# Feed-forward steps of a two-block transformer kernel: from activations standing to weights standing, with four products of 512 columns ahead of four of 256 in each block

## The reference

```python
def swiglu(x, w_gate, w_up, w_down):
    return (jax.nn.silu(x @ w_gate) * (x @ w_up)) @ w_down
...
def swiglu_ffn(x, g, w_gu, w_down):
    h = rms_norm_2(x, g)
    ...
    return (jax.nn.silu(gate) * up) @ w_down
```

## Time and profile before

| what | value |
|---|---|
| median of 3 runs | 1708.65 us (1708.61 to 1708.91) |
| the profiled execution: its own time | 1708.45 us |
| its span, first to last instruction | 1706.3 us |
| TensorE products (PE) | busy 99% of the span |
| weight loads into the array (PEld) | 81% |
| VectorE (DVE), ScalarE (ACT) | 60%, 49% |
| GpSimd (POOL) | 6% |

### The profile page before, as it was taken

The page is one execution under the profiler, slowest core; times in us unless marked ns, Lnnn a source line. Parts: engine busy times, 40 slices in busy tenths (PEclk is TensorE's granted clock), DMA queues, the critical chain, the costliest instruction groups (busy, mean ns, idle before and its releaser), DMA issues.

```text
span 1706.3 us, 22051 instructions
## 1 busy us (share of the span) xinstructions
PE 1694.1 (99%) x8308; PEld 1374.5 (81%) x8308; DVE 1022.8 (60%) x1481; ACT 840.0 (49%) x1102; POOL 109.1 (6%) x141
## 2 busy tenths in 40 slices
PE   8999999999999999999999999999999999999999
PEld 6888887788888888878778888888888787788887
DVE  6444756754556454769866545554547698665454
ACT  5444565643454343566664434443435666644342
POOL 2000200200003000100011000020001010110000
PEclk9999999999999999999999999999999999999999
DMA  8555542455557555534344554565555344345542
GB/s 296 184 202 176 173 173 99 166 193 196 180 190 232 195 185 184 197 107 159 131 136 170 189 197 175 195 229 198 176 192 195 104 156 138 129 171 194 197 172 99
DMA packets 69805, 299.87 MB, mean 176 GB/s; under 512 B 5408, under 2 KB 7680, under 8 KB 44512
## 3 DMA queue, kind: packets, MB, share of 16 engines
q1 hardware_dynamic: 66752, 291.52, 49.1%
q0 software_dynamic: 2688, 7.19, 1.4%
q10 hardware_dynamic: 288, 0.10, 0.0%
HBM read 297.74 MB, written 1.05 MB: 175 GB/s over the span
## 4 chain that ended last, share of the span: by engine, by line
PE 98%; DVE 1%; ACT 0%; DMA 0%; issue 0%; POOL 0%; ACTq 0%
PE ps L547 13%; PE ps L545 13%; PE ps L546 13%; PE ps L609 9%; PE ps L611 9%; PE ps L610 9%; PE ps L818 6%; PE ps L820 6%; PE ps L819 6%; PE ps L566 2%; PE ps L567 2%; PE ps L593 2%; PE ps L908 1%; PE ps L986 1%; PE ps L353 1%; PE ps L569 1%
## 5 line engine op out<-in xcount | busy, mean ns | idle before, releaser
L260 DVE TENSOR_TENSOR w_lo<-raw,w_hi 128x2048 fp32r<-128x2048 f32 x275 | 625.0, 2291 | 217.0 <-ACT w_hi L253 216.8
L253 ACT ACTIVATE w_hi<-raw 128x2048 fp32r<-128x2048 f32 x275 | 520.5, 1913 | 59.7 <-PE ps L820 32.5
L545 PE MATMUL ps<-w_hi,aT_hi 128*128 128x512 f32 x960 | 379.4, 395 | 0.0
L547 PE MATMUL ps<-w_hi,aT_lo 128*128 128x512 f32 x960 | 374.6, 390 | 0.0
L546 PE MATMUL ps<-w_lo,aT_hi 128*128 128x512 f32 x960 | 373.9, 389 | 0.0
L703 ACT ACTIVATE tmp<-ps,stats 128x256 f32<-128x256 f32 x132 | 62.6, 474 | 578.9 <-PE ps L547 568.6
L746 DVE TENSOR_TENSOR tmp<-tmp,ps 128x256 f32<-128x256 f32 x132 | 55.6, 421 | 337.4 <-ACT tmp L703 337.2
L609 PE MATMUL ps<-w_hi,act_hi 128*128 128x512 f32 x576 | 226.7, 394 | 0.1
L611 PE MATMUL ps<-w_hi,act_lo 128*128 128x512 f32 x576 | 224.4, 390 | 0.0
L610 PE MATMUL ps<-w_lo,act_hi 128*128 128x512 f32 x576 | 224.3, 389 | 0.0
L547 PEld LDWEIGHTS ps<-w_hi,aT_lo 128*128 128x128 f32 x960 | 180.2, 188 | 38.4
(11 more groups left out here) (296 smaller groups left out, 1605.5 us busy)
## 6 DMA issues: line engine op xcount, KB each, us to landing
raw<-in_ffn_units SPq DMA_DIRECT2D x197, 1024.0 KB, 5.0
raw<-in_w_in SPq DMA_DIRECT2D x34, 1024.0 KB, 5.2
raw<-in_w_gate SPq DMA_DIRECT2D x24, 1024.0 KB, 5.2
raw<-in_w_out SPq DMA_DIRECT2D x12, 1024.0 KB, 4.9
qk_t<-in_nsa_cmp_w POOLq DMA_DIRECT2D x8, 512.0 KB, 5.8
raw<-in_w_br_b SPq DMA_DIRECT2D x4, 1024.0 KB, 5.1
raw<-in_w_br_a SPq DMA_DIRECT2D x2, 1024.0 KB, 4.8
raw<-in_w_br_c SPq DMA_DIRECT2D x2, 1024.0 KB, 5.6
```

Of the source, the lines that this page charges most:

```text
L253: nc.scalar.activation(w_hi[w][:, :], raw[k][:, :], ACT.Copy).then_inc(hi_ready, 1)
L260: nc.vector.tensor_tensor(w_lo[w][:, :], raw[k][:, :], w_hi[w][:, :].bitcast(F32), ALU.subtract)\
L545: nc.tensor.matmul(dst, aT_hi[:, a, toks], hi[:, k, :], start=a == 0, stop=False)
L547: last = nc.tensor.matmul(dst, aT_lo[:, a, toks], hi[:, k, :], start=False, stop=a == KC - 1)
```

## The change

Step 0 of each part stays as it is. In steps 1 to 10 the roles are exchanged:

- A block is 128 hidden columns of gate or of up; a step has four (gate, up, gate, up), each with a bank of its own. The weights stand in the array, and the activations of all 256 tokens move. `aT` now holds both parts side by side, so one product with `w_hi` moves 512 columns (256 of `aT_hi`, 256 of `aT_lo`), and one with `w_lo` moves the 256 of `aT_hi`. For each half of the channels a block has four products of 512 and then four of 256.
- The bank then holds `hi*hi + lo*hi` and `hi*lo` side by side. DVE adds the two halves with a reduction (`summed`), which also brings them into SBUF.
- The result already has hidden columns on the partitions: no transposes, but for those of step 0. `rstd` now varies along the free axis, so once per part it is turned into rows of 256 numbers (`pe_rstd_rows`, a copy by ACT), and DVE multiplies the gate by it.
- The four banks of a step are the same in each step (4 to 7; in step 1 it is 2, 3, 6, 7). So TensorE waits at the start of a step until all four blocks of the last have been summed (`gu_summed`), and in step 1 the down product of tile 1 waits for the blocks in banks 2 and 3.
- In `pe_pv` the second key tile's product comes ahead of the first's.

```diff
-        def pe_gate_up(pe, n, slot, par, t, kh):
...
-            for k in range(KC // 2):
-                a = kh * (KC // 2) + k
-                nc.tensor.matmul(dst, aT_hi[:, a, toks], hi[:, k, :], start=a == 0, stop=False)
-                nc.tensor.matmul(dst, aT_hi[:, a, toks], lo[:, k, :], start=False, stop=False)
-                last = nc.tensor.matmul(dst, aT_lo[:, a, toks], hi[:, k, :], start=False, stop=a == KC - 1)
+        def pe_gate_up(pe, ph, s, like, between=None):
+            u0, n0 = ph["u0"], ph["n0"]
+            if like != 1:
+                pe.wait_ge(gu_summed, 4 * s + 4 * n0)
+            for kh in range(2):
...
+                for j, c in enumerate((0, STEP_F, P, STEP_F + P)):
+                    dst = gu_bank(like, j)
+                    for k in range(KC // 2):
+                        a = kh * (KC // 2) + k
+                        nc.tensor.matmul(dst, hi[:, k, c:c + P], aT[:, :, a, :], start=a == 0, stop=a == KC - 1,
+                                         skip_group_check=True)
+                    for k in range(KC // 2):
+                        a = kh * (KC // 2) + k
+                        mm = nc.tensor.matmul(dst[:, 0, :], lo[:, k, c:c + P], aT_hi[:, a, :], start=False,
+                                              stop=a == KC - 1, skip_group_check=True)
...
+        def pe_rstd_rows(pe, ph):
+            for t in range(NT):
+                wait_rstd(pe, ph, t)
+                last = nc.tensor.transpose(ps[:, RSTD_BANK, t * P:(t + 1) * P],
+                                           rstd(ph, t).broadcast_to([P, P]), ident)
...
+            def summed(dst, f, j):
+                wait_block(dve, ph, s, j)
+                bank = gu_bank(like, j)
+                nc.vector.tensor_reduce(dst[:, f, :], bank.rearrange("p w s -> p s w"), AX.X, ALU.add)\
+                    .then_inc(gu_summed, 1)
+                dve.wait_ge(gu_summed, 4 * s + (4 * ph["n0"] + j + 1))
+            def gate(f):
+                summed(gate_t, f, 2 * f)
+                nc.vector.tensor_tensor(gate_t[:, f, :], gate_t[:, f, :], rstd_rows, ALU.mult).then_inc(gate_scaled, 1)
+            def up(f):
+                summed(up_t, f, 2 * f + 1)
+                dve.wait_ge(silu_ready, 2 * s + (2 * s0 + f + 1))
+                nc.vector.tensor_tensor(up_t[:, f, :], up_t[:, f, :], gate_t[:, f, :], ALU.mult).then_inc(act_ready, 1)
```

More of the change, by code:

```diff
@@ L592, in pe_act_transposes, with wait_block @@
+                mm.then_inc(unit_used, 1)
+                if kh == 0 and between:
+                    between()
+        def wait_block(eng, ph, s, j):
+            if j < 3:
+                eng.wait_ge(gu_done, 3 * s + (3 * ph["n0"] + j + 1))
+            else:
+                eng.wait_ge(unit_used, 3 * s + (ph["u0"] + 1))
+        def pe_act_transposes(pe, ph, t):
+            pe.wait_ge(act_ready, 2 * ph["s0"] + t + 1)
             for f in range(2):
-                last = nc.tensor.transpose(act_t_psum(par, t)[:, f, :], sg[par][:, t, f * P:(f + 1) * P], ident)
+                last = nc.tensor.transpose(act_t_psum(t)[:, f, :], sg[:, t, f * P:(f + 1) * P], ident)
@@ L621, in pe_down @@
             pe.wait_ge(act_lo_ready, 2 * s + 2 * ph["s0"])
-            pe_rows(pe, n, (3 * like + ph["u0"] + 1) % W_SLOTS, act_hi[par], act_lo[par], 0, first, False)\
-                .then_inc(unit_used, 1)
+            if first:
+                pe.wait_ge(rstd_rows_ready, ph["ffn_before"] + 1)
+            for t in range(NT):
+                if first and t == 1:
+                    pe.wait_ge(gu_summed, 4 * (ph["n0"] + 1) + 2)
+                mm = pe_rows(pe, n, (3 * like + ph["u0"] + 1) % W_SLOTS, act_hi[par], act_lo[par], 0, first, False, (t,))
+            mm.then_inc(unit_used, 1)
         def next_of(ph):
@@ L700, in split @@
                     split_hi(act, n)
[L702 to L710, removed]
@@ L711, in act_step @@
-            if first:
-                wait_rstd(act, ph, 0)
-            else:
-                split(1)
-            act.wait_ge(gu_t0_done, s + (s0 + 1))
-            silu(0)
[L717 to L721, removed]
-            act.wait_ge(unit_used, 3 * s + (u0 + 1) if not first else u0 + 2)
-            if first:
-                wait_rstd(act, ph, 1)
+            if not in_loop and s == 0:
+                wait_rstd(act, ph, 0)
+                act.wait_ge(gu_t0_done, ph["ffn_before"] + 1)
+                for t in range(NT):
+                    if t:
+                        act.wait_ge(unit_used, u0 + 2)
+                        wait_rstd(act, ph, 1)
+                    nc.scalar.activation(sg[:, t, :], gu(t)[:, 0, :], ACT.Silu, scale=rstd(ph, t)).then_inc(silu_ready, 1)
+                return
@@ L725, in act_step @@
+            split(2)
+            split(3)
+            silu(0)
+            hi(0)
             silu(1)
+            hi(1)
             if last:
-                hi(s, par, 0)
-            if not first:
-                split(3)
-            if last:
-                hi(s, par, 1)
                 split_hi(act, ph["u_end"] + 1)
@@ new lines, in dve_step @@
+            split(1)
+            if like == 1:
+                for t in range(NT):
+                    dve.wait_ge(act_hi_ready, 2 * s0 + t + 1)
+                    toks = slice(t * P, (t + 1) * P)
+                    nc.vector.tensor_tensor(act_lo[0][:, :, toks], act_t_psum(t), act_hi[0][:, :, toks].bitcast(F32),
+                                            ALU.subtract).then_inc(act_lo_ready, 1)
+                dve.wait_ge(rstd_rows_ready, ph["ffn_before"] + 1)
+            split(2)
+            dve.wait_ge(act_lo_ready, 2 * s + 2 * s0)
@@ L764, in dve_step @@
+            gate(0)
+            if like != 1 and not last:
+                split(3)
+            up(0)
+            if like == 1:
+                split(3)
+            gate(1)
+            lo(0)
+            up(1)
+            lo(1)
             if last:
-                lo(s, par, 0)
-            if not first:
                 split(3)
-            if last:
-                lo(s, par, 1)
                 split_lo(dve, ph["u_end"] + 1)
@@ L983, in pe_pv @@
                 pe.wait_ge(att_pt_dve if hh else att_pt_act, B + 1)
-            for kt in range(NT):
+            for kt in (1, 0):
                 for hh in range(2):
```

104 lines of the change are left out of this document (52 added, 52 removed).

## The result

The change takes 1703.28 us (1703.04 to 1704.11), the kernel before 1708.63: a ratio of 0.9969, 95% interval 0.996 to 0.9978. It is faster by 0.3%; 0.8% was forecast, and the time lies 0.3 us outside the range. One of the eight runs of the kernel before was a slow one (1873.42 us), and the ratio is of fast runs alone. The profiled execution has a span of 1701.3 us.

The account below looks back on a forecast made before the run. TensorE's own products were taken as the bound. Savings of 14.6 (loop steps) and 3.1 (ends), less 2.6 (step 1) and 1.4 (opening stalls), make 13.7 us off 1708.45: 1694.75, median 1695.0 us; range 1692 to 1703.

Parts of the forecast that it names:

- the switch back from 256 to 512: In gate and up, eight times a step: taken to cost 0, bounded from above by 0.11 us each.
- the forecast step: Steps 2 to 10: 11.09 us gate and up plus 5.44 down, kept as 16.54 us, against 16.81 before.
- The rival that the switch costs: Switch from 256 back to 512, 480 times: at 0.03 us each 1709 us, at 0.11 us 1748; chance 0.05.
- The other rivals for the loop: Among them, products of 256 not covering their operand load: 2.2 us more a step, 1829 us; chance 0.03.
- the gap behind a wait: First two products behind a wait, 0.34 us apart against 0.2267: gave the switch back's upper bound of 0.11 us.
- the forecast's own signs of being wrong: A loop step over 16.7 us, reductions near 1 us, or PE waiting in the loop.
- The sign for the step: Loop steps: the forecast counts as wrong if one takes over 16.7 us, where 16.54 was forecast.
- The opening stall: Start of step 2 in each part: TensorE waits for DVE's last reduction, 0.21 to 0.25 us; six cost 1.4 us.
- the rival of longer hand-overs: Opening and end: 0.1 us more per link between engines or dependent operations, giving 1701 us; chance 0.2.
- Step 1 up to its down product: Step 1's gate and up products with six transposes at 0.71 us: 11.81 us.
- The end: End of each part: two pairs of transposes go, 0.52 us, 3.1 us in six; `act_lo` in time with 0.46 us slack.
- One price of a rival: Reduction at 1.36 us, twice the forecast: 26 us lost, 1721 us, loop still holding with 0.3 us slack; chance 0.08.

Follow-up runs that it names:

- far order: The change with all 16 products of 512 in a half of the channels, then its 16 of 256 (reversed in the second half of steps 2 to 9): 1696.32 us.
- strict alternation: The change with each product of 512 followed at once by its product of 256, 32 returns a step: 1709.19 us, ratio 1.0004 to the kernel before.
- pairs: The change with the products of two blocks gathered, 8 of 512 and then 8 of 256, so 4 returns a step: 1703.03 us.
- groups of two: The change with two products of 512, then two of 256, and so on, 16 returns a step: 1698.26 us, ratio 0.9941 to the kernel before.

## Why the prediction was wrong

**The step that failed** is the sentence on the switch back from 256 to 512: "I take 0". Gate and up come to 11.20 us instead of 11.09, nine times a part, and the down product behind them to 5.47 or 5.49 instead of 5.44, eight times: 0.99 + 0.38 = 1.37 us a part, 8.2 us in six. The miss is 8.3 us (1703.28 less 1695.0); that the two agree so well is chance, as the other terms below show, but this one is by far the largest. It was shown by moving products alone: the far order gave the forecast step, the strict alternation ate the gain. The rival that the switch costs was named, with a chance of 0.05 and a price of 0.03 us each for no gain; spread over 480 returns the measured cost is 0.017. The other rivals for the loop did not come up. A bound looked for in one row, the gap behind a wait, was the wrong kind of row: the cost lies in the distances of the five to nine products behind it, and the earlier trace rows were read for one distance only.

None of the forecast's own signs of being wrong came up: a step took 16.70 us and not more, the reductions 0.69, and PE did not wait in the loop. The sign for the step was too wide: 0.16 us over the forecast in each of 60 steps is 9.6 us, more than the range allows.

**The opening stall** was forecast at 0.21 to 0.25 us and took 0.40: 6 x 0.17 = 1.0 us. The last reduction came at 17.45 instead of 17.29. DVE's own chain, from the split to that reduction, took 8.61 us, the forecast's 8.65; it began 0.20 late, because ACT was busy when its copy fell due and because DVE followed ACT by 0.10 us and not 0.03. PE then started 0.14 us behind DVE, not 0.06. So the rival of longer hand-overs was right in two links between engines, not in the waits of DVE for itself.

**The other terms.** Step 1 up to its down product: 5.59 + 0.57 + 5.69 = 11.85 us, forecast 11.81 (the six transposes took 0.57, not 0.71, and the products more). Its down product took 0.03 us more without the stall (5.47). The end: 0.47 us less, forecast 0.52; `act_lo` came in time, and pairs showed how little was to spare. The reduction: 686 ns, forecast 680. Silu reads SBUF now and takes 420 ns, forecast 474; the copy for `act_hi` 419, forecast 380. The loop's chain on DVE hid as forecast. The attention loop: nothing, as forecast. Step 1 and the end make another 0.7 us in six parts, so the terms come to 8.2 + 1.0 + 0.7 = 9.9 us, 1.6 more than the miss. Some 0.9 us of it came back between the parts (0.1 to 0.3 us each time, of which no term of the forecast speaks; why was not followed up). Another 0.4 us is that the time of an execution lies 1.97 us over its span in the change and 2.15 before, and that the profiled execution of the change is at its median and not 0.2 below. The rest is rounding. One price of a rival does not follow from its own numbers: with a reduction of 1.36 us the loop's slack of 2.7 us is used up by 4 x 0.68 = 2.7, and 0.3 us is not left. Nothing hung on it.

The forecast rested on the rows. The Trainium skill (TensorE: Matmul & The Clock Gate, Back-to-back issue gap) has a formula for an isolated product, by which one of 256 columns would be estimated at 109.2 ns. The far order, with 32 in a row, has 120, so the trace does not agree. The Trainium skill (TensorE: Matmul & The Clock Gate, The mechanism) also says that a load overlaps running products only when the row group differs. Here too the trace does not agree: in the far order 32 loads of 0.19 us, all over 128 rows, start every 0.12 us beside the products.

The kernel gains less than it could because of its order, not because of the roles: with the orders of TensorE and of DVE's step 1 changed, the forecast's 1695 is reached and passed (1693.94).

## What to carry to other kernels

Where TensorE is the bound and products of two widths are mixed, gather those of one width as far as the banks and the engines behind allow, and read the distances of all the products behind a change of width, not the first alone: 15 ns for eight products is 0.5% of the whole. Halfway gathering is no sure gain: groups of two (a step of 16.60 us) beat groups of four and of eight (16.70, 16.63), and they let each block complete as early as in the change, so a few lengths are worth a run. Before gathering, ask which block becomes complete later and who waits for it: at the end of a part 0.90 us of delay against 0.46 us of slack ate the whole gain of gathering pairs. And a wait that is added between steps has its cost where the engine behind it catches up, in the first step; there, put the long operation that is not yet due last.

## What the runs showed of the hardware that was not expected

Products of 512 columns behind products of 256 are longer than 227 ns, five of them where nothing disturbs them (233, 236, 228, 233, 231) and nine behind the transposes of the kernel before; in strict alternation single ones reach 241. The first products of 256 behind wide ones are shorter than 120 (113, 119). It does not depend on how the moving operand lies (one run or two), on DVE's reads of PSUM, or on whether the loads overlap. It does depend on the lengths of the groups, and not in one direction: 1 + 1 costs 25 ns for eight products, 2 + 2 costs 7, 4 + 4 costs 16. What in the chip makes this pattern is open; a rule that gives 7 and 16 was not found, and no run here looks inside.
